# A hybrid encoder layer on one core: rotation without products, query norms applied to the scores, gelu tiles before gates

## The reference

```python
xn = rms_norm(x, attn_norm)
z = xn @ w_in
q, k, v, xl, yg, gl = jnp.split(z, IN_SPLITS, axis=-1)
q = partial_rope(rms_norm(q.reshape(B, T, N_HEADS, HEAD_DIM), q_norm), positions)
k = partial_rope(rms_norm(k.reshape(B, T, N_KV_HEADS, HEAD_DIM), k_norm), positions)
...
s = jnp.einsum('bnqkgd,bnskd->bnkgqs', q, k).astype(jnp.float32) * ATTN_SCALE
m = jnp.maximum(jnp.max(s, axis=-1, keepdims=True), sink)
p = jnp.exp(s - m)
den = jnp.sum(p, axis=-1, keepdims=True) + jnp.exp(sink - m)
...
xc = conv_b + xp[:, 0:T] * conv_w[0]        # and three more taps
r = sigmoid(xc @ w_rg + b_rg); i = sigmoid(xc @ w_ig + b_ig)   # in blocks of 64
a = jnp.exp(-LRU_C * r * softplus(-lru_lambda))
b = sqrt(1 - a * a) * i * xc                # then h = a * h + b along time
lru_branch = (h * jax.nn.gelu(yg)) @ w_lru_out
```

## Time and profile before

| | us |
|---|---|
| median of 3 runs | 1684.65 |
| lowest and highest | 1684.54, 1687.44 |
| the profiled execution | 1689.49 |
| its span | 1687.7 |

### The profile page before, as it was taken

One profiled execution on the slowest core, in us unless ns is written; L12 is line 12 of the kernel. 1 busy time (PEld: TensorE's weight loads), 2 busy tenths in 40 slices (PEclk: granted clock), 3 DMA queues, 4 the chain that ended last, 5 costly groups with the idle time before them and its releaser, 6 DMA issues. The chain is left out here.

```text
span 1687.7 us, 28388 instructions
## 1 busy us (share of the span) xinstructions
PE 1631.9 (97%) x11242; PEld 1539.6 (91%) x11242; DVE 1055.2 (63%) x1648; ACT 621.5 (37%) x1310; POOL 962.1 (57%) x685
## 2 busy tenths in 40 slices
PE   7899999999999999999898999999999999999999
PEld 4799989988889898898897989999999999998998
DVE  6687774964747555667889778333333334869685
ACT  5444551243343524424234334333333334333242
POOL 5665652222123131377785717877777777786876
PEclk9999999999999999999999999999999999999999
DMA  5011122133123131264441512222242222373744
GB/s 189 28 62 64 58 68 90 64 86 104 55 87 77 62 103 57 98 216 167 153 154 60 196 51 84 94 77 77 83 166 97 76 77 77 140 257 122 254 141 148
DMA packets 72771, 182.21 MB, mean 108 GB/s; under 512 B 14704, under 2 KB 26416, under 8 KB 72000
## 3 DMA queue, kind: packets, MB, share of 16 engines
q1 hardware_dynamic: 51376, 159.13, 27.0%
q10 hardware_dynamic: 21264, 21.27, 4.3%
HBM read 131.36 MB, written 49.28 MB: 107 GB/s over the span
## 5 line engine op out<-in xcount | busy, mean ns | idle before, releaser
L566 PE MATMUL bank<-xh,wsh 128*128 128x264 f32 x2170 | 623.4, 287 | 23.1 <-POOL wsl L542 8.0
L566 PE MATMUL bank<-xh,wsl 128*128 128x264 f32 x2170 | 619.5, 285 | 0.0
L566 PE MATMUL bank<-xl,wsh 128*128 128x264 f32 x2170 | 618.9, 285 | 0.0
L566 PEld LDWEIGHTS bank<-xh,wsh 128*128 128x128 f32 x2170 | 411.4, 190 | 26.5 <-issue 17.3
L566 PEld LDWEIGHTS bank<-xl,wsh 128*128 128x128 f32 x2170 | 411.5, 190 | 0.2
L566 PEld LDWEIGHTS bank<-xh,wsl 128*128 128x128 f32 x2170 | 411.4, 190 | 0.0
L566 PE MATMUL bank<-acth,wh 128*128 128x352 f32 x960 | 320.8, 334 | 4.6 <-POOL actl L498 3.7
L566 PE MATMUL bank<-acth,wl 128*128 128x352 f32 x960 | 311.7, 325 | 0.0
L566 PE MATMUL bank<-actl,wh 128*128 128x352 f32 x960 | 310.2, 323 | 0.0
L490 POOL TENSOR_SCALAR wh<-wraw 128x512 fp32r<-128x512 f32 x100 | 81.1, 811 | 397.2 <-PE bank L566 376.8
L542 POOL TENSOR_TENSOR wsl<-praw,wsh 128x512 fp32r<-128x512 f32 (+1 forms) x157 | 243.0, 1548 | 82.0 <-ACT wsh L1151 82.0
(11 more groups left out here) (173 smaller groups left out, 2397.0 us busy)
## 6 DMA issues: line engine op xcount, KB each, us to landing
praw<-in_weights SPq DMA_DIRECT2D x34, 1024.0 KB, 4.9
wraw<-in_weights SPq DMA_DIRECT2D x52, 512.0 KB, 3.3
h_scratch<-ev SPq DMA_DIRECT2D x44, 264.0 KB, 2.0
acc<-h_scratch SPq DMA_DIRECT2D x4, 2112.0 KB, 11.6
ev<-x_scratch SPq DMA_DIRECT2D x6, 1056.0 KB, 4.9
spare<-x_scratch SPq DMA_DIRECT2D x6, 1056.0 KB, 5.1
praw<-in_weights SPq DMA_DIRECT2D x8, 768.0 KB, 5.0
ta_scratch<-tg ACTq DMA_DIRECT2D x24, 176.0 KB, 1.9
```

Source lines behind the costliest of these rows:

```text
L566: return nc.tensor.matmul(*args, **kw)
```

## The change

**LRU groups.** The order of units is x, x, gelu, gelu, gates, gates. `split` takes only the 256 used columns of a gate unit. TensorE does both gelu tiles, then both columns' gate products; ScalarE follows it; VectorE makes `xcl` before the tails, and in the first group scales x tile 1 before the first convolution.

**Values.** The first four tiles are accumulated side by side in four banks, half a unit at a time.

**Keys and queries.** Units of keys and queries are split with their columns in another order (`turned`): the halves of each group of 16 features stand in different halves of the partitions, so a feature's partner is 64 partitions off. Rope tables, gains, cached keys and the key outputs are turned by their transfers. VectorE forms the sine part with two products over 64 partitions that read `qsb` of the other half (`halves`). Keys keep their norm, with sums two blocks late (`k_sums`) and the root one block later than before. Queries are rotated only; their squares go into the attention's output tile `ot`, and at pass 18 of the group `q_sums` makes 17 small products, squares as weights and two columns of `heads` as moving data, which gives each query row's sum in the rows of the scores. Root and reciprocal follow (`q_root`, `q_inverse`); the exponential takes it as its scale. `nm0` becomes two instructions of one column.

**Order of steps.** Steps 0 and 1 stand at passes 66 and 77, step 2 and later where they were (94, then each 11).

**Transfers.** The three cache transfers move to SyncE's queue, behind x; the keys' are now two, turned. `cs` is loaded by SyncE in two transfers when the gates have ended. A group's keys and values take nine transfers instead of seven; a last key block six stores instead of four.

```diff
-START_MM, SLOT_MM = 72, 11
+START_MM, SLOT_MM, LATE_MM = 66, 11, 6
...
+FRONT_UNITS = (0, 1, 2, 4, 3, 5)
...
                 for half in range(2):
                     c = slice(half * UW // 2, (half + 1) * UW // 2)
-                    nc.gpsimd.tensor_scalar(wh[:, u, c], wraw[:, u, c], 1.0, 0.0, ALU.mult, ALU.add).then_inc(split_done, 1)
+                    if i < V_PAIR and i % 3 == 2:
+                        c = slice(half * P, (half + 1) * P)
+                    raw, high, low = wraw[:, u, c], wh[:, u, c], wl[:, u, c]
+                    if turned:
+                        raw, high, low = turn(raw), straight(high), straight(low)
+                    nc.gpsimd.tensor_scalar(high, raw, 1.0, 0.0, ALU.mult, ALU.add).then_inc(split_done, 1)
...
+            vjobs = [plan.take() for t in range(V_FIRST)]
+            for half in range(4):
+                weights(half // 2, half % 2)
+                for job in vjobs:
...
-                mm(aux0[:, 0:BW], blkones, qsq[:, k % 2, :], start=True, stop=True).then_inc(ss_done, 1)
-                wait(pe, rot_used, base + k)
-                mm(aux1[:, 0:BW], perm, qsb[:, k % 2, :], start=True, stop=True).then_inc(rot_done, 1)
...
+            def k_sums(k, b, after):
                 wait(pe, free[b], after)
+                wait(pe, std_done, k)
+                mm(aux0[:, 0:BW], heads[:, :], qsq[:, k % 2, :], start=True, stop=True).then_inc(ss_done, 1)
...
+            def q_sums(g, job):
+
+                wait(pe, free[job.bank], job.after)
+                wait(pe, std_done, 6)
+                wait(pe, qroot_done, 2 * g)
+                wait(pe, ot_done, AU * g)
+                for u in range(AU):
+                    q, _, q0 = unit_shape(u)
+                    i = mm(aux0[0:2 * q, 2 * u:2 * u + 2], qsquares(g)[:, 2 * q0:2 * (q0 + q)], heads[:, 0:HD:HD // 2],
+                           start=True, stop=True)
+                i.then_inc(qss_done, 1)
...
-                wait(act, rot_done, base + k - 1)
-                wait(act, t1_done, base + k - 1)
-                f(qsq[:, k % 2, :], bank[job.bank][:, 0:BW], ACT.Square)
-                f(qsb[:, k % 2, :], bank[job.bank][:, 0:BW], ACT.Identity, scale=gain).then_inc(free[job.bank], 1)
...
+                wait(act, cos_done, base + k - 1)
+                f(qsb[:, k % 2, :], ps, ACT.Identity, scale=gain).then_inc(copied, 1)
+                if base == 0:
+                    wait(act, ss_done, k - 1)
+                    f(qsq[:, k % 2, :], ps, ACT.Square).then_inc(free[job.bank], 1)
...
+            for j in range(12):
+                qk_copy(j // 6 * 6, j % 6, (kgain, qgain)[j // 6])
+                if 2 <= j < 8:
+                    k_root(j - 2)
+                if 3 <= j < 9:
+                    store_k(j - 3)
...
-                        f(pr[0:2 * q, r, h, 0:k], sbank[i % 2][0:2 * q, h * P:h * P + k], ACT.Exp, scale=HD ** -0.5,
+                        f(pr[0:2 * q, r, h, 0:k], sbank[i % 2][0:2 * q, h * P:h * P + k], ACT.Exp,
+                          scale=qinv[0:2 * q, 0, i, h:h + 1],
...
-                V.tensor_tensor(rt2[:, :], aux1[:, 0:BW], cs[:, 1, x], ALU.mult).then_inc(rot_used, 1)
-                V.tensor_tensor(rt1[:, :], qsb[:, k % 2, :], cs[:, 0, x], ALU.mult).then_inc(t1_done, 1)
...
+                stt(rt2[0:HD, :], qsb[HD:P, k % 2, :], -1.0, cs[HD:P, 1, x], ALU.mult, ALU.mult).then_inc(sin_done, 1)
+                stt(rt2[HD:P, :], qsb[0:HD, k % 2, :], 1.0, cs[0:HD, 1, x], ALU.mult, ALU.mult).then_inc(sin_done, 1)
+                V.tensor_tensor(rt1[:, :], qsb[:, k % 2, :], cs[:, 0, x], ALU.mult).then_inc(cos_done, 1)
...
```

More of the change, by code:

```diff
@@ L271, in blk, with turned @@
         return slice(n * BW, (n + 1) * BW)
+    def turned(rows):
+        return rows.rearrange("(a s b) t -> s a b t", s=2, b=PAIR_ROWS)
     ctx = ExitStack()
@@ L481, in _, with turn, straight, split @@
         def _(pool):
-            def split(i, u, first):
+            def turn(half):
+                return half.rearrange("p (c a s b) -> p s c a b", c=4, s=2, b=PAIR_ROWS)
+            def straight(half):
+                return half.rearrange("p (c s a b) -> p s c a b", c=4, s=2, b=PAIR_ROWS)
+            def split(i, u, first, turned=False):
                 wait(pool, raw_loaded[u], 16 * i + 16)
@@ L1357, in _ @@
             norm(2)
+            for n in range(NB):
+                scale_raw(1, n, raw_jobs[1][n])
             def skip(jobs, per_unit=NB):
@@ L1379, in lru_front @@
                 for i in range(2):
-                    if first and i == 1:
-                        for n in range(NB):
-                            scale_raw(1, n, raw_jobs[1][n])
                     wait(dve, free[jobs[i].bank], jobs[i].after)
```

257 lines of the change are left out of this document (146 added, 111 removed).

## The result

The changed kernel takes **1674.67 us** (median of 4 runs, 1673.24 to 1678.89), beside 1686.05 for the kernel before on the same chip (1684.54 to 1690.38): a ratio of 0.9927, 95% interval 0.991 to 0.9944. It is faster by 11.4 us. The forecast was 1646.5, with a range from 1638 to 1660: 28 us too low, and outside the range. The profiled execution took 1678.89 us (span 1677.0), 4.2 above its median.

What follows compares the result with a forecast made beforehand. TensorE, holding a matmul in 97% of the span, was taken as the bound: its passes plus its stands. Terms 6.7 + 1.8 + 6.7 + 17.7 + 4.7 - 0.5 - 1.7 + 2.7 = 38.1 us gave 1646.5 us, range 1638 to 1660.

Steps and rivals of the forecast that it cites:

- The first group's gates: First group's gate products: second gelu tile placed ahead removes a 4.1 us stand and 2.6 us of half clock; gain 6.7 us.
- the values with the first key half: Value tiles taken by half units end stands and half clock, gain 6.7 us; slower first key splits lose 0.5 us.
- the turned splits: GpSimd's key splits in runs of 8: a quarter longer, two halves exposed; loss 0.5 us, ends 0 and 6.
- rival C: Turned splits of key and query units outrun their cover, slower than before: 1716 us at 5 times the length; chance 0.05.
- the steps' places: Attention's first steps: step 0 six passes earlier removes TensorE's stand at step 2 in every group; gain 2.7 us.
- The rotation's 60 passes: Key and query blocks: VectorE rotates instead of TensorE's permutation products, 60 passes of 0.295 us; gain 17.7 us.
- Part 4: Query norms: 48 passes go (14.2 us), 34 small passes a group at 0.07 us come (9.5 us); gain 4.7 us.
- parts 1 and 2: Gate products and values: new orders remove TensorE's stands and half clocks; gains 6.7 and 1.8 us, then 6.7 us.
- Rival D: Stalls only move, half clocks return at gates and values, later phases catch another: 1656 to 1662 us; chance 0.07.
- signs of being wrong: Turned splits far over 2 us a half; small passes over 0.1; "ACT qstd" waits over 5; kg-load wait; gates' half clock.
- Part 5: Keys: slower turned splits lose 0.5 us; a 5.9 us block chain makes TensorE stand 3.2, before 1.5, losing 1.7.
- Part 1 in the groups 2 to 4: Gates of the later LRU groups: 2.8 us of standing and refilling go, 1.0 given back; gain 1.8 us.

Runs made afterwards that it cites:

- x_v_first_1: Changed kernel with one value tile taken first instead of four side by side, the order of before: 1679.15 us, 0.9960 of the kernel before.
- x_start72: Changed kernel with the attention steps at their old places, step 0 at pass 72 and each next 11 passes on: 1678.43 us, 0.9951 of before.
- x_wide: Changed kernel with 128 moving columns instead of 2 in each of a group's 17 small products: 1671.61 us, 0.9915 of the kernel before.
- x_wide64: Changed kernel with 64 moving columns instead of 2 in each of a group's 17 small products: 1668.70 us, 0.9889 of the kernel before.
- x_halved: Changed kernel with a group's small products in two rows, 9 at pass 18 and 8 at pass 40: 1668.32 us, 0.9881 of the kernel before.
- x_again: The changed kernel run once more with nothing edited: 1675.82 us, 0.9927 of the kernel before.
- x_keys: Changed kernel with rope tables in three blocks, ScalarE's store waits moved to the first query block, key roots ahead of copies: 1671.78 us, 0.9909 of before.
- x_cs_late: Changed kernel with the rope tables' loads issued when the first value unit is done, not when the gates are: 1680.01 us, 0.9960 of before.

## Why the prediction was wrong

**Right.** The first group's gates (6.7 us forecast, 6.7 measured); the values with the first key half (6.2, 6.2; x_v_first_1 shows the mechanism); the turned splits (forecast 0.5, measured nothing; rival C had no ground); the steps' places (2.7; 3.4 by x_start72). The rotation's 60 passes are gone, and VectorE's work for it shows in no query group's waits; it has no run of its own. These are 33 us of gain, and they arrived. The account of one group bears it out: 96.35 us before, less 24 passes of 0.295 and 0.6 at step 2, with 3.8 of small passes, 3.4 of clock and 0.4 of "DVE ot", is 96.3, and 96.1 was measured. The 6.2 of the values is luck by half a microsecond: the values alone gave 6.2 and not 6.7, and the turned splits cost nothing where 0.5 was counted.

**The step that failed most** is a term that wasn't there. Part 4 priced the small products and asked nothing of the clock behind them, though parts 1 and 2 of the same text counted half clocks as costs of stands. The earlier trace rows show half clock behind stretches in which TensorE did little, and I read them as the price of standing alone; a row of 34 two-column passes is in the busy time in full, and the clock fell in it too. It cost 11.9 us, and x_wide, x_wide64 and x_halved show it. Rival D had half clocks, but by stands, and at 10 to 16 us instead of 28. Two of the signs of being wrong that the prediction named did come: small passes over 0.1 us, and over 5 us of waits for "ACT qstd" (5.9).

**Part 4's price.** 0.07 us a pass was taken, 0.112 measured: 5.7 us. The row that I used, two loads ending 0.06 apart, is of a single pair; the starts of the same transposes stood 0.16 apart. The moving columns hardly count: 64 cost the same as two, and 128 a little more. The rule of the Trainium skill ("TensorE: Matmul & The Clock Gate", section "LDWEIGHTS (loading the stationary operand)"), 107 ns for 128 columns, was set against the trace in the prediction; the runs agree with it, at 0.112 us.

**Part 5 and the transfers.** The forecast had a stand of 3.2 us at the keys. It was 9.2 in the profile (five stands) and 6.4 in x_again (four). The length of the chain was nearly right (5.9 a block, 6.1 measured), its start was not (the root of block 0 ended 19.0 us after the values in the profile and 16.8 in x_again, 14.6 in the forecast): "has caught up when the values end" and the tables "some 10 us before they are needed" are the two sentences that failed, and they failed together. I looked at when the tables are wanted, not at who stands behind them. The wait of 1.9 us for the first queries' squares is the same lateness once more.

**Part 1 in the groups 2 to 4.** +1.8 forecast, -0.7 measured. The stand at the gates went, and two came at the next group's x tile: half a split takes 2.9 us, against 2.9 of gate products for the first half and 1.9 of x passes for the second. The prediction looked only at VectorE's and ScalarE's cover there, not at GpSimd's.

The shortfall closes: 11.9 (clock) + 5.7 (price) + 6.0 (stand at the keys) + 1.9 (squares) + 2.5 (groups 2 to 4) = 28.0, against 38.1 forecast and 10.1 measured at the end of the front. That it closes to the tenth is luck: the 1.6 us of "DVE ot" are not in it, so other terms must have given about as much more than forecast.

## What to carry to other kernels

Before many small products are put in one row on TensorE, ask what the clock does behind them: here four rows of 34 two-column passes lost 11.9 us by the clock beside the 15 us of their passes, and moving more columns than needed, or cutting the row in two, gave most of it back. When a load is moved to another queue, look at what lands behind it and not only at when it is wanted. When one engine's stall is removed, look at the engine whose slack it was.

## What was not expected of the hardware

With weights of 128 columns in fp32, a pass of 2 or of 64 moving columns costs 0.112 us, one of 128 columns 0.137, and one of 2 columns between dense passes of 352 still 0.112 on average. The granted clock fell to 1.2 GHz in the middle of a row of two-column products, and with the same row elsewhere in time one group of four kept 2.4 GHz in x_keys, x_cs_late and x_v_first_1. The chain of landing and waiting around the value stores differed by 2.4 us between two executions of the same kernel.
